# Tile-wise normalisation: the inverse deviation in PSUM instead of SBUF

## The reference, cut to what matters

```
h = concat(meta, x)                                                     # 528 x 1024
h = layer_norm(alpha*h + 0.5*swiglu(h, ffn1), ln1_g, ln1_b)             # 1st normalisation
h = layer_norm(alpha*h + hybrid_mixer(h), ln2_g, ln2_b)                 # 2nd normalisation
h = layer_norm(alpha*h + 0.5*swiglu(h, ffn2), ln3_g, ln3_b)             # 3rd, by rows
return h[:, 16:]

def layer_norm(x, g, b):
    mu  = mean(x, -1);  var = mean((x - mu)**2, -1)
    return (x - mu) * rsqrt(var + 1e-5) * g + b
```

## Time and profile before

| | |
|---|---|
| Median of three runs | 1124.44 us (1123.28 to 1125.76) |
| The profiled execution | 1123.59 us |
| Its span, first to last instruction | 1121.9 us |
| Mean granted clock of TensorE | 0.985 of full speed |
| Busy: TensorE, VectorE, ScalarE, POOL | 1079.1, 468.6, 347.4, 134.1 us |
| Multiplications L1545 | 16 |
| Reciprocals L1539 | 2 |

### The profile page before, as it was taken

How to read it: one execution, slowest core, us unless ns; L and a number is a source line. 1 busy time by engine, 2 the same in 40 slices (tenths; PEclk the granted TensorE clock), 3 DMA queues, 4 the chain that set the end, 5 groups by cost and what they waited for, 6 DMA issues and landing times.

```text
span 1121.9 us, 15986 instructions
## 1 busy us (share of the span) xinstructions
PE 1079.1 (96%) x6569; PEld 931.7 (83%) x6569; DVE 468.6 (42%) x725; ACT 347.4 (31%) x453; POOL 134.1 (12%) x98
## 2 busy tenths in 40 slices
PE   8999999999999999999988999999999999999993
PEld 7999999999999987689865568768888888888882
DVE  3332332323232253699885533553333333322235
ACT  3222322222121234434337532452223232221211
POOL 4000000000011115212313004240000000000001
PEclk9999999999999999989998999999999999999997
DMA  6424233231322323122210101223333333143311
GB/s 191 113 75 111 76 87 100 75 100 52 104 79 86 106 75 97 38 79 73 76 38 1 38 1 46 67 75 89 99 92 95 96 91 100 59 134 89 92 51 75
DMA packets 159165, 90.34 MB, mean 81 GB/s; under 512 B 6596, under 2 KB 156792, under 8 KB 159128
## 3 DMA queue, kind: packets, MB, share of 16 engines
q1 hardware_dynamic: 159128, 89.83, 28.1%
HBM read 87.72 MB, written 2.10 MB: 80 GB/s over the span
## 4 chain that ended last, share of the span: by engine, by line
PE 88%; DVE 6%; ACT 3%; POOL 2%; issue 1%; DMA 0%; DVEq 0%; SPq 0%; POOLq 0%
PE ps L919 75%; PE ps L1054 4%; POOL xl L484 2%; PE ps L1328 2%; PE ps L1308 1%; PE ps L1319 1%; DVE x L1545 1%; DVE zrow L1503 1%; PE ps L1336 1%; DVE sil L1539 1%; PE ps L1116 1%; ACT whi L617 1%; DMA xin<-in_x 0%; DVE x L1528 0%; PE ps L1218 0%
## 5 line engine op out<-in xcount | busy, mean ns | idle before, releaser
L919 PE MATMUL ps<-xl,whi 128*128 128x264 f32 (+1 forms) x1264 | 350.9, 330 | 8.9 <-POOL xl L484 8.0
L919 PE MATMUL ps<-xh,whi 128*128 128x264 f32 (+1 forms) x1264 | 356.1, 331 | 2.7 <-DVE wlo L1412 1.6
L919 PE MATMUL ps<-xh,wlo 128*128 128x264 f32 (+1 forms) x1264 | 353.3, 329 | 0.0
L919 PEld LDWEIGHTS ps<-xl,whi 128*128 128x128 f32 x1264 | 212.4, 190 | 36.4 <-POOL xl L484 16.1
L919 PEld LDWEIGHTS ps<-xh,whi 128*128 128x128 f32 x1264 | 212.8, 189 | 30.0 <-issue 5.9
L919 PEld LDWEIGHTS ps<-xh,wlo 128*128 128x128 f32 x1264 | 213.8, 189 | 21.7 <-issue 0.2
L1403 DVE TENSOR_TENSOR wlo<-wraw,whi 128x2048 fp32r<-128x2048 f32 (+1 forms) x81 | 171.5, 2117 | 144.0 <-ACT whi L617 144.0
L617 ACT ACTIVATE whi<-wraw 128x2048 fp32r<-128x2048 f32 (+1 forms) x89 | 152.4, 1712 | 129.6 <-PE ps L919 123.8
L919 PE MATMUL ps<-hh,whi 128*128 128x264 f32 (+1 forms) x528 | 141.5, 322 | 0.0
L919 PE MATMUL ps<-hl,whi 128*128 128x264 f32 (+1 forms) x528 | 141.2, 321 | 0.0
L919 PE MATMUL ps<-hh,wlo 128*128 128x264 f32 (+1 forms) x528 | 140.4, 320 | 0.0
(11 more groups left out here) (217 smaller groups left out, 873.8 us busy)
## 6 DMA issues: line engine op xcount, KB each, us to landing
wraw<-in_ffn_w_gate SPq DMA_DIRECT2D x44, 512.0 KB, 4.0
wraw<-in_ffn_w_up SPq DMA_DIRECT2D x43, 512.0 KB, 5.2
wraw<-in_ffn_w_down SPq DMA_DIRECT2D x32, 384.0 KB, 3.4
wraw<-in_ffn_w_down SPq DMA_DIRECT2D x32, 320.0 KB, 3.8
wraw<-in_w_in SPq DMA_DIRECT2D x19, 512.0 KB, 4.7
wraw<-in_w_out SPq DMA_DIRECT2D x8, 512.0 KB, 4.0
xin<-in_x SPq DMA_DIRECT2D x2, 1024.0 KB, 6.1
out<-zrow SPq DMA_DIRECT2D x8, 256.0 KB, 2.0
```

The lines of the kernel that those rows point to most:

```text
L919: mm = pe.matmul(ps[:, b + e, 0:width], w, mov, start=(first and n == 0), stop=(last and n == 2))
```

## The change

The reciprocal writes to `bank(6, p)`, the PSUM columns that held the mean square, and the multiplications read it there. The views of both become those of two banks where there are 528 columns. The mean square is read for the last time by L1533, ahead of the reciprocal, and no product is written to these banks before the first unit of the next stage is done. Instructions, their number, their order and their waits stay as they are.

```diff
                 dve.wait_ge(s["sd_done"], 1)
-                dve.reciprocal(var, flat(sil[:, 1, :], p)).then_inc(s["rstd_done"], 1)
+                rstd = bank(6, p)
+                dve.reciprocal(rstd, cols(sil[:, 1, :], p)).then_inc(s["rstd_done"], 1)
                 dve.wait_ge(s["rstd_done"], 1)
                 for k in range(KT):
                     if 2 <= k + 1 < KT:
                         centre(k + 1)
                     dve.wait_ge(s["sub_done"], k + 1)
-                    dve.tensor_tensor(flat(x[:, k, :], p), flat(x[:, k, :], p), var, ALU.mult).then_inc(s["norm_done"], 1)
+                    z = cols(x[:, k, :], p)
+                    dve.tensor_tensor(z, z, rstd, ALU.mult).then_inc(s["norm_done"], 1)
```

## The result

| | before | changed |
|---|---|---|
| Median | 1123.82 us (6 runs, 1121.79 to 1125.76) | 1118.18 us (6 runs, 1115.50 to 1119.20) |
| Profiled execution, its span | 1123.59, 1121.9 us | 1119.20, 1117.5 us |
| Ratio of the runs | | 0.9949 (95%: 0.9933 to 0.9964) |

The changed kernel is faster by 5.6 us in the medians, 4.0 to 7.5 by the interval.

The account below looks back on a forecast made before the run. TensorE bounds the kernel (96% busy), waiting in both normalisations on VectorE and POOL, which exclude each other over the SBUF port. Gains 2.0 + 1.9 = 3.9 us, so 1124.44 - 3.9 = 1120.5 us, range 1118.6 to 1123.2.

Parts of the forecast that it names:

- What bounds the kernel, and the port: TensorE busy 96%; in both normalisations it waits while POOL and VectorE instructions with two SBUF inputs exclude each other.
- Part (a): Two reciprocals, one per normalisation, write PSUM instead of SBUF; claimed extra cost 0.
- Rival 3: Reciprocals lose a two-column mode by writing PSUM: 6.5 us more, 2.6 slower overall, 1127.0 us; chance 0.05.
- Part (b): Sixteen normalisation multiplications read PSUM: 0.69 us each whatever POOL does; gains 2.0 us in the first normalisation, 1.9 second.
- rival 2: Multiplications in both normalisations still wait for POOL because x is in SBUF: no change, 1124.4 us; chance 0.04.
- the estimate of 65 ns more for each: Skill's fixed PSUM source cost on each multiplication; would make the summed gain 0.1 us smaller.
- Rivals 1 and 4: Rival 1: moved weight split delays POOL in both normalisations, 1124.8 us; 0.09 including costlier reciprocal. Rival 4 has its line.
- Rival 4: Split doesn't delay POOL: TensorE's last pair 3.9 us earlier per normalisation, 7.8 us, 1116.6; 0.06 including what lies towards it.
- The sum for the first normalisation: TensorE's last low pair starts at 430.9 instead of 432.80: 1.9 us, plus 0.1 for no idle start, 2.0 us.
- so I cost the clock at nothing: Granted clock 0.9 or more in the slices of both normalisations, so no clock effect was priced.
- The second place: Second normalisation, 512 columns: TensorE's last low pair starts at 740.8 instead of 742.71, gain 1.9 us.
- The absolute time and the range: Whole kernel: 1124.44 - 3.9 = 1120.5 us, range 1118.6 to 1123.2.

Follow-up runs that it names:

- A: Trace of the unchanged kernel before the edit, the one the prediction read; profiled execution 1123.59 us, first normalisation 38.49 us from reciprocal to reduction.
- D: Third of four further traces of the kernel before, no edit; first normalisation 39.99 us from reciprocal to reduction.
- E: Last of four further traces of the kernel before, no edit; first normalisation 39.98 us from reciprocal to reduction.
- B: First of four further traces of the kernel before, no edit; first normalisation 38.83 us from reciprocal to reduction.
- C: Second of four further traces of the kernel before, no edit; first normalisation 39.92 us from reciprocal to reduction.

## Why the prediction was right or wrong

- **What bounds the kernel, and the port: right.** What VectorE and POOL exclude each other from is an instruction with both inputs in SBUF (1251 against 685 ns for one line in one trace), and as L1541 showed later, also one in a mode of two columns.
- **Part (a), the reciprocal at nothing: right.** 3.454 and 3.354 us to PSUM against 3.444 and 3.346 to SBUF. Rival 3, the lost mode, falls with it.
- **Part (b), the multiplications: right.** 700 and 683 ns; the split was issued 12.1 us behind the reciprocal (12.2 by the sum), took 3.03 us ("about 3") and fell on POOL's k = 5, which took 3.20 ("about 3.1"); the others took 1.3. The chain went to ScalarE and then POOL. With them falls rival 2, and so does the estimate of 65 ns more for each, from the table of the Trainium skill ("VectorE: DVE Perf Modes", section on the TRN2 errata): 0.70 us with PSUM against 0.71 for the first undisturbed one in SBUF.
- **Rivals 1 and 4: both fell.** POOL meets the split once, and it costs 1.8 us there, as the kernel with the split held back showed (place 17.84 for 19.66). Rival 4's lead of 3.9 us in each place is what that kernel shows (21.73 to 17.84, 21.40 to 17.49), but most of what it has over the changed kernel is spent on waiting for the split.
- **The sum for the first normalisation: the mechanism right, the size off.** The step that failed is "so I cost the clock at nothing". It looked at the clock in trace A alone. The sum gave 2.0 us, and A against the first trace of the changed kernel gives 2.07, but the mean of the traces is 3.1, since four of six of the old form ran 1.1 to 1.5 us slower behind TensorE's wait for POOL, at half clock. A was one of the two that didn't, and one trace can't show that. The second place was given 1.9 and measured 2.06.
- **The absolute time and the range: too narrow below.** The forecast stood on a median of three runs, 1124.44; with six it is 1123.82, and on other occasions 1122.2 and 1122.0. Of the 2.3 us between forecast and measured median, 0.6 are this and 1.7 the gain (5.6 for 3.9). Of the 1.7, the two places without the clock give 0.2 and the halved clock 1.0; the last 0.5 no trace accounts for, and it is well within the interval of the gain. The range allowed 1.1 us more gain and 0.8 for the median, and 1118.18 lies 0.4 us below it.

## What to carry to other kernels

Where VectorE and POOL work side by side, look at each VectorE instruction for a second input in SBUF, or a single one in the mode of two columns; an operand moved to an idle PSUM bank frees both engines and cost nothing here. Then ask which instruction has the port next: here the weight split behind the loop took back 1.8 us in each place, and that loss went only when it was put where POOL had been standing still, with the last two-column instruction in its way moved to PSUM as well. A wait of TensorE can cost more than its length, by the clock behind it (1.1 to 1.5 us here behind a wait of 1.65 or 2.3), and one trace doesn't show how often: read the granted clock around each wait in several executions before pricing it.

## What the runs showed that I had not expected

- A halved granted clock behind a wait of TensorE comes in some executions of the same program and not in others. After the same wait of 1.65 us for POOL it stayed at 1.00 in A, and fell in D and E; after 2.3 us it stayed in B and fell in C. It cost 1.1 to 1.5 us there, 1.2 in the first place of the kernel with the variance in PSUM, and 2.6 in the second place with the split on POOL alone. Why the new form was spared in all its four traces, although TensorE waits 1.65 us for POOL's k = 5 in it, I have not shown, nor that it was more than luck. In the slices before that wait TensorE stands still for 0.25 to 0.3 us per slice in the old form and not at all in the new.
- Giving POOL a share of the work cost as much as the whole edit had won (1.0002) where it held up a single instruction of 0.43 us on the path, and with the variance in PSUM the same share was a gain over the changed kernel: 0.9930 against its repeat's 0.9966, intervals apart, though its first measurement (0.9949) overlaps.
- VectorE writing 512 or 528 columns of PSUM, which no row of before shows, is as fast as into SBUF where no mode is lost: 3.45 us for the reciprocal and 0.72 for the difference (0.71 into SBUF). L1541 went from 0.43 to 0.72 us, the price of two columns at a time.
